# A bidirectional recurrent mixer on one core: key columns without padding, pairs of half-height gram products, and more gate blocks computed inside it

## What is computed

```python
def rwkv_step(S, inp):
    r_t, w_t, k_t, v_t, kk_t, a_t = inp
    sa = jnp.einsum('dbhij,dbhj->dbhi', S, -kk_t)
    S = (S * w_t[..., None, :] + sa[..., :, None] * (kk_t * a_t)[..., None, :]
         + v_t[..., :, None] * k_t[..., None, :])
    y = jnp.einsum('dbhij,dbhj->dbhi', S, r_t)
    return S, y
...
def second_block(x, norm1_g, w_in, ...):
        h = rmsnorm(x, norm1_g[l])
        p = h @ w_in[l]
        p_rwkv, q, k, v, gate_logits = jnp.split(p, IN_SPLITS, axis=-1)
        y_a = rwkv7_bidirectional(p_rwkv, ...) @ w_o_rwkv[l]
        y_b = neighbourhood_attention_2d(q, k, v, q_gain[l], k_gain[l], rpb[l]) @ w_o_na[l]
        g_a, g_b = jnp.split(jax.nn.sigmoid(gate_logits + b_gate[l]), 2, axis=-1)
        x = x + (g_a * y_a + g_b * y_b) @ w_out[l]
        x = x + hierarchical_moe(rmsnorm(x, norm2_g[l]), ...)
```

## Time and profile before

| | |
|---|---|
| median of 3 runs | 2486.81 us (2480.73, 2486.81, 2487.56) |
| profiled execution | 2481.65 us, its span 2479.9 us |
| PE busy in the span | 2220.9 us, 90% |
| DVE, POOL, ACT busy | 1017.9, 881.5, 788.7 us |
| products of `products` in the mixer (L655 to L657) | 3 x 152 |
| mixer, second merge | about 1503 to 1939, 1939 to 2060 us |

### The profile page before, as it was taken

How to read it: one execution, slowest core, us unless ns; L and a number is a source line. 1 busy time by engine, 2 the same in 40 slices (tenths; PEclk the granted TensorE clock), 3 DMA queues, 4 the chain that set the end, 5 groups by cost and what they waited for, 6 DMA issues and landing times. The chain is left out here.

```text
span 2479.9 us, 30354 instructions
## 1 busy us (share of the span) xinstructions
PE 2220.9 (90%) x11597; PEld 1722.9 (69%) x11597; DVE 1017.9 (41%) x1686; ACT 788.7 (32%) x1237; POOL 881.5 (36%) x788
## 2 busy tenths in 40 slices
PE   7999897999987988999996988789999898599994
PEld 5888776777776876888875655678888687444441
DVE  3222355676753463332245554465674215311112
ACT  4333242443433434333324444222121423111110
POOL 4333146565652444444321102335444343000001
PEclk9999899999998999999997999899999999699998
DMA  5433032333323433323305302111111333799994
GB/s 163 108 77 87 11 101 73 89 93 80 88 52 97 130 128 119 101 90 96 118 17 104 80 29 82 29 30 29 23 31 22 101 91 130 297 409 423 423 423 168
DMA packets 287448, 300.30 MB, mean 121 GB/s; under 512 B 78192, under 2 KB 248432, under 8 KB 277680
## 3 DMA queue, kind: packets, MB, share of 16 engines
q1 hardware_dynamic: 278584, 266.80, 34.1%
q0 software_dynamic: 5280, 19.18, 2.1%
q10 hardware_dynamic: 3456, 12.58, 1.2%
HBM read 322.01 MB, written 26.84 MB: 141 GB/s over the span
## 5 line engine op out<-in xcount | busy, mean ns | idle before, releaser
L2607 PE MATMUL moe_bank<-ex_wgu,Y 128*64 128x512 f32 x768 | 171.0, 596 | 1.6 <-ACT Y L2654 1.6
L655 PE MATMUL gdn_bank<-hh,gdn_ws 128*128 128x512 f32 x368 | 161.1, 438 | 9.3 <-POOL gdn_ws L885 9.3
L885 POOL TENSOR_TENSOR gdn_ws<-gdn_wr,gdn_ws 128x1024 fp32r<-128x1024 f32 x44 | 105.7, 2408 | 117.4 <-ACT gdn_ws L1179 117.3
L657 PE MATMUL gdn_bank<-hh,gdn_ws 128*128 128x512 f32 x368 | 145.9, 397 | 0.0
L656 PE MATMUL gdn_bank<-hl,gdn_ws 128*128 128x512 f32 x368 | 145.3, 395 | 0.0
L2607 PEld LDWEIGHTS moe_bank<-ex_wgu,Y 128*64 128x64 f32 x768 | 66.2, 138 | 100.9 <-issue 100.9
L2579 POOL DMA_INDIRECT hT<-token_rows,rows x24 | 22.8, 951 | 304.1 <-PE moe_bank L2592 236.5
L2285 DVE TENSOR_TENSOR ff_hes<-hT,ff_hes 128x1024 fp32r<-128x1024 f32 x16 | 23.5, 1469 | 207.5 <-ACT ff_hes L2244 207.5
L655 PE MATMUL ff_bank<-ff_wds,ff_hes 128*128 128x512 f32 x256 | 99.7, 389 | 1.8 <-DVE Y L2301 1.8
L656 PE MATMUL ff_bank<-ff_wds,ff_hes 128*128 128x512 f32 x256 | 99.6, 389 | 0.0
L657 PE MATMUL ff_bank<-ff_wds,ff_hes 128*128 128x512 f32 x256 | 99.6, 389 | 0.0
(11 more groups left out here) (590 smaller groups left out, 6008.8 us busy)
## 6 DMA issues: line engine op xcount, KB each, us to landing
ex_wgu<-in_w_gate_e SPq DMA_DIRECT2D x48, 1024.0 KB, 19.1
ex_wgu<-in_w_up_e SPq DMA_DIRECT2D x48, 1024.0 KB, 18.5
ex_wd<-in_w_down_e SPq DMA_DIRECT2D x48, 1024.0 KB, 21.3
Y<-in_w_in SPq DMA_DIRECT2D x48, 512.0 KB, 3.9
gdn_wr<-in_w_in SPq DMA_DIRECT2D x44, 512.0 KB, 4.2
wu<-in_w_ff SPq DMA_DIRECT2D x16, 1024.0 KB, 11.7
ff_wd<-in_w_ff SPq DMA_DIRECT2D x16, 1024.0 KB
expert_rows<-Y ACTq DMA_DIRECT2D x24, 512.0 KB
```

The source lines that it names most:

```text
L655: pe.matmul(bank, left(0, l), right(0, r), start=(start and n == 0), stop=False)
L657: ins = pe.matmul(bank, left(1, l), right(0, r), start=False, stop=(stop and n == len(pairs) - 1))
L885: pool.tensor_tensor(ws[:, r % 2, 1], raw[r], ws[:, r % 2, 0], ALU.subtract).then_inc(s.lo, 1)
L2607: ins = pe.matmul(bank[2 + j][half, :], hgT[:, j, k, half], w[:, e, k], start=(k == 0), stop=(k == KT - 1))
```

## The change

1. `columns` makes one column operand `B` of 128 rows per direction with one `tensor_tensor`, `key_columns` likewise; `Kz` is half as large. No half is zero any more.
2. The grams use rows 64e to 64e + 63 of both operands. `gram_n` still runs one head at a time. `gram_t` takes the two heads together, alternating between them chunk by chunk, into two banks.
3. Jobs 0, 1, 3 and 4 are `pe.transpose`, as job 2 was.
4. The mixer computes 14 gate blocks, not 4: two in period -1, two at the head of each of the periods 0 to 2, ahead of `x_mm` (`fill(16)`), six in period 3, of which two are at the head. ACT copies the logits to one buffer (`gst`), SP stores them in DRAM. The sigmoid, with its bias, moves into the merge.
5. The second merge is now `merge_from_logits`, with a bias; `merge_phase` is gone.

```diff
+        for g, us in enumerate((2, 2, 2, 2, 6)):
+            u0 = 2 * g
+            order += [(None, u) for u in range(u0, u0 + us)]
+            if 0 < g < PAIR:
+                order += [(LORA + 3 * g + j, None) for j in range(3)]
+            begun.append(len(order))
...
+            def store(u):
+                sp.wait_ge(s.gs, u + 1)
+                sp.dma_start(gates_dram[u // 2, :, u % 2, :], gst[:]).then_inc(s.gate_out, 16)
...
             for p in periods:
                 i, g = stages(p)
+                b0 = begun[p + 1]
+                if p == -1:
+                    load(b0)
+                    load(b0 + 1)
+                    load(b0 + 2)
+                    store(0)
+                    load(b0 + 3)
+                    store(1)
+                    load(b0 + 4)
+                else:
+                    store(2 * p + 2)
+                    load(b0 + 3)
+                    store(2 * p + 3)
+                    load(b0 + 4)
+                    load(b0 + 5)
+                if i is not None and g is not None:
+                    load(b0 + 6)
+                    load(b0 + 7)
                 if g is not None:
-                    for q in range(3 * g + 6, 3 * g + 9):
-                        load(q)
                     sp.wait_ge(s.ntm, 4 * g + 4)
...
-                if i is not None:
+                b0 = begun[p + 1]
+                if i is None:
+                    for q in range(b0, b0 + 4):
+                        lower(q)
+                else:
+                    lower(b0 + 2)
+                    lower(b0 + 3)
                     whole(i)
                     mask_b(i, 0)
...
-            def gram(out, left, right):
+            def gram(out, left, right, e):
                 for n in range(NT):
                     c0 = slice(n * P, (n + 1) * P)
-                    ins = pe.matmul(out[:, c0], left[:, c0], right[:, c0], start=True, stop=True)
+                    ins = pe.matmul(out[:, c0], left[hd(e), c0], right[hd(e), c0], start=True, stop=True)
...
-                gram(bank[2 + m % 4], Kz[:, d, e] if kind else Bz(d, e), ft[:, g % 2, d, A_ if kind == 1 else R_]).then_inc(s.gr, 1)
+                left, right = Kz[:, d] if kind else B(d), ft[:, g % 2, d, A_ if kind == 1 else R_]
+                for n in range(NT):
+                    c0 = slice(n * P, (n + 1) * P)
+                    for e in range(2):
+                        ins = pe.matmul(bank[2 + (m + e) % 4][:, c0], left[hd(e), c0], right[hd(e), c0], start=True, stop=True)
+                        if n == NT - 1:
+                            ins.then_inc(s.gr, 1)
...
+                    src = B(d) if t < 2 else Kz[:, d]
                     for n in range(NT):
-                        for e in range(2):
-                            src = (Bz(d, e) if t < 2 else Kz[:, d, e])[:, n * P:(n + 1) * P]
-                            ins = pe.matmul(b[:, n * P + HR * e:n * P + HR * e + HR], src, G.c("ident", HR * e, HR * e + HR), start=True, stop=True)
+                        ins = pe.transpose(b[:, n * P:(n + 1) * P], src[:, n * P:(n + 1) * P], G.c("ident"))
...
                 if i is not None:
+                    fill(16)
                     x_mm(i, 0)
...
             def gate(u):
-                act.wait_ge(s.proj, first_gate + u + 1)
-                act.activation(gates[:, u], bank[(first_gate + u) % 2][:, :], ACT.Sigmoid, bias=gb[:, u // 2, u % 2:u % 2 + 1]).then_inc(s.gs, 1)
+                q = gate_at[u]
+                act.wait_ge(s.proj, q + 1)
+                if u:
+                    act.wait_ge(s.gate_out, 16 * u)
+                act.activation(gst[:], bank[q % 2][:, :], ACT.Copy).then_inc(s.gs, 1)
...
+                if i is not None:
+                    gate(2 * p + 2)
+                    higher(b0 + 2)
+                    gate(2 * p + 3)
+                    higher(b0 + 3)
...
                     decays(g, 2)
                     if i is not None:
                         middle(q + 2)
-                        higher(q + 4)
+                        higher(b0 + 6)
+                    else:
+                        gate(1)
+                        higher(b0 + 3)
                     decays(g, 3)
...
-                for e in range(2):
-                    ins = dve.scalar_tensor_tensor(Bz(d, e), af[:, d, g, :], half[e], Kz[:, d, 0], ALU.mult, ALU.mult)
-                ins.then_inc(s.bz, 1)
+                dve.tensor_tensor(B(d), af[:, d, g, :], Kz[:, d], ALU.mult).then_inc(s.bz, 1)
...
-                merge_phase(nc, G, "m2", A.w_o_rwkv[0], A.w_o_na[0], w_in2, (N_GA, N_GB), A.w_out_2[0], A.gate_bias, (hh, hl), (2, 3), 2, (2, 1, (0, 1, 2, 3)))
+                merge_from_logits(nc, G, "m2", A.w_o_rwkv[0], A.w_o_na[0], block(wi2, N_GB + (KT - 1) * P), A.w_out_2[0], (hh, hl), gates_dram,
+                                  [at(1), at(2)], [at(0)[:, 0:4], at(0)[:, 4:8]], gate_room, 1, (0, 1), A.gate_bias)
```

More of the change, by code:

```diff
@@ L1603, in sigmoids @@
                     act.wait_ge(sg_ready[q % 2], 16 * (q // 2) + 16)
-                    act.activation(sg[:, q % 2], sg[:, q % 2], ACT.Sigmoid).then_inc(s.sig, 1)
+                    if gate_bias is None:
+                        act.activation(sg[:, q % 2], sg[:, q % 2], ACT.Sigmoid).then_inc(s.sig, 1)
+                        return
+                    if q == 0:
+                        act.wait_ge(s.bias_in, 16)
+                    for n in range(2):
+                        ins = act.activation(sg[:, q % 2, n, :], sg[:, q % 2, n, :], ACT.Sigmoid, bias=gb[:, q, n:n + 1])
+                    ins.then_inc(s.sig, 1)
                     return
@@ L3149, in rwkv_phase, with emptied @@
         inv_rows = inv_dram.rearrange("(b r) (i j) -> b i r j", b=NBLK, i=HB)
-        first_gate = LORA + 3 * PAIR
-        nblocks = first_gate + 4
-        gates = xr[:, 2048:4096].rearrange("p (u t) -> p u t", u=4)
+        order = [(o, None) for o in range(2 * LORA)]
+        begun = [len(order)]
+        for g, us in enumerate((2, 2, 2, 2, 6)):
[4 more added lines that the diff above has]
+            begun.append(len(order))
+        nblocks = len(order)
+        number = {o: q for q, (o, u) in enumerate(order) if u is None}
+        gate_at = {u: q for q, (o, u) in enumerate(order) if u is not None}
+        units = len(gate_at)
+        def emptied(q):
+            o, u = order[q]
+            return (s.shift, o + 1) if u is None else (s.gs, u + 1)
         def chunk(d, st):
@@ L3245, in _ @@
                 sp.dma_start(dst, view).then_inc(s.gate_in, 16)
+            sp.wait_ge(s.yz, 6 * PAIR)
+            sp.wait_ge(s.gate_out, 16 * 4)
+            for dst, q in logits_back:
+                sp.dma_start(dst, gates_dram[q]).then_inc(s.gate_in, 16)
+            for u in range(units - 4, units):
+                store(u)
             sp.wait_ge(s.uu, 8 * (PAIR - 1) + 7)
@@ L3599, in _ @@
                 if g is not None:
-                    for m in range(4):
-                        gram_t(g, m)
+                    gram_t(g, 0)
+                    gram_t(g, 2)
                 if g is None:
@@ L3770, in _ @@
                 if g is None:
-                    gate(2)
+                    gate(units - 2)
                 if i is not None:
```

317 lines of the change are left out of this document (61 added, 256 removed).

## The result

| | before | after |
|---|---|---|
| median, us | 2483.93 | 2465.51 |
| lowest to highest (10 runs each) | 2478.85 to 2488.43 | 2453.85 to 2478.08 |
| profiled execution, its span | 2481.65, 2479.9 | 2464.16, 2462.0 |

The ratio is 0.9922, 95% interval 0.9905 to 0.9939. So the change makes the kernel faster by 18 us, not by the 42 forecast, and 2465.5 lies above the range. The runs of the changed kernel also lie over 24 us, those of before over 10.

The account below looks back on a forecast made before the run. PE bounds, but level with the inverse chain between `systems` and `x_mm`. Terms -53.0 + 2.5 + 0.3 + 8.8 - 0.5 = -41.9 us take 2481.65 to 2439.75, forecast as 2440 us, range 2425 to 2460.

Parts of the forecast that it names:

- 1, the merge: Second merge: loses 10 gate blocks and keeps 2; 54.5 us less, 1.5 us charged for late loads, -53.0 us.
- The loop through DRAM: Second merge: logits, weights and their parts just fit, 9.5 to 10.8 of 10.9 us per two blocks; 1.5 us charged.
- 2 and 3, jobs and `gram_t`: Between `systems` and `x_mm`: plain transposes take 5.4 us less PE a period, half-height `gram_t` in turns 3.75 us less.
- Rival (a): Grams: the array's two halves don't overlap; +18 us, 2458; chance 0.20.
- rival (d): Grams: every change of half drains the array; +71 us, 2511; chance 0.04.
- 3, `gram_n`: Mixer: half-height `gram_n`, with its changes of shape, costs 1.25 us more a period.
- 4, the columns: Mixer: one DVE column operation instead of two cuts PE's waits by 2.9 us per period, perhaps 0.5 us left.
- 5, the head of period -1: Two gate blocks, their 16 steps fitting into gaps and beside slow groups, cost +0.8 us; the whole head +2.5.
- 5, period 0: From `systems` to `x_mm`: PE work of 30.35 us, then a wait of some 4 us for the inverses.
- 6, POOL: Low parts ahead of `whole` make PE 2.0 us late in periods 1 to 3, 2.8 in period 0: +8.8 us.
- Rival (c): Heads of periods: POOL's low parts make PE wait 6 us a period; +15 us, 2455; chance 0.11.

Follow-up runs that it names:

- experiment 7: The changed kernel with POOL's `whole` ahead of its low part and, in period -1, ACT's high part behind the decays: 2445.40 us, ratio 0.9836.
- experiment 5: The changed kernel again, unchanged, on another chip: 2467.53 us, ratio 0.9931.
- experiment 4: The changed kernel with eight extra products a period in periods 0 to 2, ahead of the first two `gram_n`: 2444.40 us, ratio 0.9832.
- experiment 8: The changed kernel with POOL's `whole` first, ACT's high part behind the decays, and eight extra products a period in periods 0 to 2: 2432.58 us.
- experiment 10: The kernel before with one column operation, half-height grams in turns, plain transposes and eight extra products a period in periods 0 to 2: 2486.99 us (2496.97 without).
- experiment 12: The changed kernel with padded columns, full-height grams and old jobs put back, and POOL's `whole` ahead of its low part: 2477.59 us, ratio 0.9962.
- experiment 11: The kernel before with only eight extra products a period in periods 0 to 2 added: 2490.38 us, ratio 1.0020.
- Experiment 3: The changed kernel with POOL's `whole` ahead of the second low part at the head: 2448.48 us, ratio 0.9843.

## Why the prediction was too low

The sum was -41.9 us and the profiled execution shows -17.5. By the prediction's own steps:

- **1, the merge**: -53.0 predicted, -53.3 measured. The loop through DRAM does not bound it: all of its 57.6 us are PE busy.
- **2 and 3, jobs and `gram_t`**: right. 36.48 us from store to `x_mm` at the full clock where the prediction had 36.35, and the pair 1.09 us. (Half of 10.9 is 5.4, not 5.3; a job costs 0.5 to 0.6 us, not 0.45. Both are small.) Rival (a), no overlap, and rival (d), a drain at each change, are excluded by that row.
- **3, `gram_n`**: right. From 1874.35 to the start of what follows `solved` (1878.11; before 1839.53 to 1842.70) it is 3.75 us after and 3.17 before for two of them, 1.2 us a period (I had 1.25).
- **4, the columns**: mis-sized. Half of the wait stayed, 1.14 + 0.68 = 1.8 us a period instead of 0.5: DVE is later than one operation. 1.3 us in each of three periods, 3.8 us with the small rest.
- **5, the head of period -1**: mis-sized. The 16 steps did not fit into the gaps: from the first `cums` (1562.13) to the first gram (1581.71) 19.6 us instead of 15.2, so +4.4 and not +0.8. The gates ahead of the decays on ACT made the second gram's wait 3.3 us (experiment 7), and to the store (29.6 us) the mean clock was 0.83: the three grams behind that wait took 4.77 us, where before they took 2.92. +7.9 instead of +2.5.
- **5, period 0**: "PE waits some 4 us for the inverses" was right, 3.5; but `x_mm` came 1.3 us later. The last set of the inverses' DMAs took 5.26 us there and 4.02 in the control (experiment 5), where `x_mm` came after 33.64 us, as before; so this belongs to the one execution, not to the change.
- **6, POOL**: right in place and in size, 2.4 us a period (I had 2.0 and 2.8). Rival (c) asked for 6.
- **The step that failed is the one that is not in the sum**: every duration was taken at the full clock from `x_mm` on, and the granted clock was taken as given by the windows of before (0.97 over period 0 and what follows). Periods 0 and 1 of the kernel after, against its own period 2, lose 6.4 and 6.3 us from `x_mm` to the store and 2.4 and 2.5 from there to `x_mm`; before lost 2.5 and 1.6. That is 17.6 - 4.1 = 13.5 us.

Together 13.5 + 5.4 + 3.8 + 1.3 = 24.0 of the 24.4 missing.

None of the rivals named was this one. That the clock belongs in the sum is shown by experiments 4, 8 and 10, where PE was given more to do and the time went down by 21, 13 and 10 us. What is not settled is the condition. The same waits and the same grams leave the clock alone in period 2, and full-height code has falls too: at this place in experiment 12, and in experiment 11, between the store and `x_mm`, two that last 7 and 10 us. At the grams the waits alone do not make a long fall: in periods 1 and 2 of experiment 12 they are longer (1.8 and 1.59 us against 1.14 and 0.68) and each fall is over within 4 us. No run has half-height grams without these waits and without extra products, so it isn't shown whether the height alone would do it, or only both together. Experiment 3 took out only waits that lie some 28 us ahead of the grams, and in its one profile the falls are shorter; its surplus over the waits, 7 us, is put down to the clock by that profile alone.

What the change should have had with it is one line on POOL: `whole` ahead of the low part whose weights come late. With it the change is worth 36 us, and with ACT's order and the extra products 52.

## What to carry to other kernels

Two edits that are worth nothing each can be worth much together: one opens room that runs into a wait, the other fills it. When PE is loaded to the brim, put the granted clock of each stretch into the sum as a term of its own with both ends priced, and if a stretch of small products falls to the lower level, try a few products whose results nobody reads; they cost next to nothing where PE would wait anyway. On an engine with a fixed order, never place work whose input comes late ahead of work whose result is awaited.

## What I had not expected of the hardware

- Extra products make a kernel that PE bounds faster: 2465.5 to 2444.4 us with 24 more, 2445.4 to 2432.6 with the orders mended, and the runs spread over 7 us instead of 24.
- The clock fell inside a stretch in which PE waited no longer than 1.14 us at a time (`solved` 1.00 us, then 1.97), and stayed down for 17 us; in full-height code, at the same place and behind waits of 1.8 and 1.6 us, it came back within 4.
- Half-height fp32 products of 128 columns follow each other at 0.102 us on one half, at 0.068 when the halves take turns, where full-height ones need 0.113. A group of eight of them between full-height groups costs, with the products behind it, 0.29 us more than the same at full height: a short group on one half alone does not pay.
